# Expert activations of the last 192 tokens as row dot products on VectorE, the dense U product for 384 tokens, in a diff-attention, pooling and PEER layer

## The chip, the cores and the metric

The kernel runs on one core of a Trainium2 chip. The metric is the device time of one execution in microseconds (us); the times shown are of single executions, and their median is what a change is measured by.

## What is computed

One layer of a hybrid decoder for 512 prompt tokens and 64 sample tokens (576 in all, model width 2048): projection, differential attention over a prompt and over paged caches, a pooling branch, gates, output projection, and then the PEER mixer, which the change touches. All numbers are fp32.

```python
def peer_block(h, w_q, sub_keys, u, v):
    N = h.shape[0]
    q = (h @ w_q).reshape(N, PEER_HEADS, 2, PEER_HALF)
    s = jnp.einsum('nhcd,hckd->nhck', q, sub_keys).astype(jnp.float32)
    sv, si = lax.top_k(s, PEER_TOPK)
    cand = (sv[:, :, 0, :, None] + sv[:, :, 1, None, :]).reshape(N, PEER_HEADS, PEER_TOPK * PEER_TOPK)
    cidx = (si[:, :, 0, :, None] * PEER_KEYS + si[:, :, 1, None, :]).reshape(N, PEER_HEADS, PEER_TOPK * PEER_TOPK)
    top_s, top_p = lax.top_k(cand, PEER_TOPK)
    experts = jnp.take_along_axis(cidx, top_p, axis=-1)
    gate = jax.nn.softmax(top_s, axis=-1)
    act = jax.nn.gelu(jnp.einsum('nd,nhkd->nhk', h, u[experts]).astype(jnp.float32), approximate=False)
    return jnp.einsum('nhk,nhkd->nd', (gate * act).astype(h.dtype), v[experts])
```

There are 8 heads, 128 x 128 = 16384 experts, and 16 chosen experts per head, so 128 per token. u and v are 16384 x 2048 (134 MB each). The output is y = h + PEER(norm(h)), normed once more.

## The kernel before

Five engines run programs of their own, written out by hand and joined by semaphores. Every projection multiplies 128-column tiles of a weight with the activations of all tokens. An fp32 product is made of three fp32r ones: weight and activation are split into a rounded part (`w_hi`, `act_hi`; ScalarE casts) and a rest (`w_lo`, `act_lo`; VectorE subtracts), and TensorE adds hi*hi, hi*lo and lo*hi in PSUM.

**Queries.** 16 tiles of `w_peer_q` (`G_PQ`) give the queries `q_ev`; `key_scores` compares each with its sub-keys in fp32, and `best` on VectorE takes the 16 best of 128.

**The U stage.** For all 576 tokens the product with all 16384 rows of u is made, in `N_U` = 128 tiles of 128 experts. Per tile SP loads 1 MB of u into `w_raw` (four DMAs), VectorE transposes it by halves into `turned` (`turn`) and subtracts (`u_low`), ScalarE casts (`u_high`), TensorE runs `expert_tile`: 16 contraction steps, each three products by two halves of 288 tokens, 96 matmuls. ScalarE takes GELU out of PSUM (`gelu`), and SP stores it to `gelu_dram`. Buffers hold two tiles. Beside tiles 0 to 29 VectorE chooses the experts of five token blocks, in pieces that stand between half tiles (`low_half`); TensorE turns the choice (`turn_selected`) so that `iaT`, `ibT`, `gT` hold first index, second index and gate for each token and choice. Beside tiles 30 to 77 the gate matrix of the first `TV` = 384 tokens is made, 8 tokens a tile: VectorE writes one-hots (`one_i`, and `gate_j` twice, with the gate's rounded part and its rest), TensorE multiplies them (`gate_matrix`, 8 matmuls of 256 columns), ScalarE copies and VectorE adds the two parts into `gmat`, and POOL stores it to `gmat_dram` by 32 tokens.

**The value stage.** For 384 tokens the 128 tiles of v are multiplied with GELU times gate (`a_back`, `g_back`), dense, two tiles at a time into `main` (`take_sum`). The last `N_SP` = 192 tokens are done sparsely: POOL gathers for each token its 128 GELU values, one element for each partition (`gather_cells`), and its 128 rows of v (`gather_rows`, 1 MB a token), and TensorE adds up the weighted rows four tokens at a time (`expert_sums`).

Order around the change: VectorE's program is one_hots, merge_gates, u_low and turn, by halves; ScalarE's is u_high of the next tile, GELU, gate copies. At the end of the U stage SP waits for the gate stores, reloads the residual into `main` (whose memory `gmat` shares), loads the first GELU and gate tiles, then v tiles.

```python
def u_low(n, s, i, last=False):
    dve.wait_ge(u_hi, n * 2 + (i + 1))
    v.tensor_sub(w_lo[s][:, 8 * i:8 * i + 8, :], turned[i][:, :, :],
                 w_hi[s][:, 8 * i:8 * i + 8, :].bitcast(F)).then_inc(u_lo, 1)
    if not last:
        dve.wait_ge(u_lo, n * 2 + (i + 1))
        turn(n + 1, 1 - s, i)
```

## Time and profile before

| | us |
|---|---|
| median of 3 executions (4904.4 to 4916.15) | 4909.15 |
| the profiled execution, its own time | 4921.65 |
| its span in the trace | 4919.6 |
| first 30 tiles of the U stage, 1852.5 to 2238.9 | 386.4 |
| tiles 31 to 126, GELU to GELU, 2251.8 to 3526.7 | 1274.9 |
| TensorE busy (matmul) | 4749.3 |
| VectorE busy | 2807.5 |
| ScalarE busy | 1217.3 |
| GpSimd (POOL) busy | 780.0 |

Positions are microseconds from the span's start. A matmul's own duration in a row overlaps with its neighbours', so the time that one takes is read from the distance of the starts. "Idle before" a group and its releaser tell what the engine waited for. The share of DMA is the mean busy share of the 16 DMA engines.

### The profile page before, as it was taken

How to read it: one execution, taken by the hardware profiler on the slowest of the kernel's cores; microseconds unless marked ns; L12 is line 12 of the kernel's file. 1: busy time of each engine (PE TensorE's matmuls, PEld its weight loads, DVE VectorE, ACT ScalarE, POOL GpSimd, SP SyncE). 2: the span in 40 equal slices, each digit the busy share in tenths (PEclk: the TensorE clock that was granted, in tenths of full speed). 3: DMA queues.
4: the chain of work that ended last, by engine and by line, in shares of the span. 5: the costliest groups of instructions: out<-in, count | busy, mean ns of one | idle time of the engine just before them, and what ended most of it. 6: DMA issues, size and time to landing. Idle time of an engine off the chain costs nothing.

```text
span 4919.6 us, 84579 instructions
## 1 busy us (share of the span) xinstructions
PE 4749.3 (97%) x35079; PEld 4510.0 (92%) x35079; DVE 2807.5 (57%) x5183; ACT 1217.3 (25%) x1483; POOL 780.0 (16%) x768
## 2 busy tenths in 40 slices
PE   8999999999999899999999999999999999999997
PEld 8999888888999899999999999999988888888887
DVE  3332643223343668878888863333366666776667
ACT  3212533322121212222222221212222222222223
POOL 1010012320000000000011000000054334434430
PEclk9999999999999999999999999999999999999999
DMA  6333246763445334434555554344488778877873
GB/s 191 104 112 99 64 158 216 235 202 102 134 128 144 71 72 105 109 100 118 131 141 141 133 133 109 102 106 107 162 318 304 303 302 302 310 265 302 305 298 110
DMA packets 474042, 842.18 MB, mean 171 GB/s; under 512 B 45201, under 2 KB 307345, under 8 KB 431512
## 3 DMA queue, kind: packets, MB, share of 16 engines
q1 hardware_dynamic: 400272, 502.55, 33.9%
q0 software_dynamic: 67968, 325.20, 19.0%
q10 hardware_dynamic: 5520, 10.49, 0.7%
q8 instruction: 199, 3.26, 0.3%
q14 instruction: 83, 0.68, 0.0%
HBM read 739.48 MB, written 94.14 MB: 169 GB/s over the span
## 4 chain that ended last, share of the span: by engine, by line
PE 80%; DMA 8%; DVE 6%; issue 3%; ACT 2%; SPq 1%; ACTq 0%; DVEq 0%
PE pair L1795 61%; PE pair L2218 10%; DMA v_raw<-in_peer_v_dram 7%; PE pair L1759 2%; DVE v_lo L1672 2%; PE pair L2199 2%; DVE main L1690 2%; ACT v_hi L1086 1%; PE pair L2152 1%; PE pair L1966 1%; ACT w_hi L776 1%; PE pair L1831 1%; PE pair L2009 1%; SPq L537 0%; PE pair L2106 0%
## 5 line engine op out<-in xcount | busy, mean ns | idle before, releaser
L1795 PE MATMUL pair<-act_hi,w_hi 128*128 128x288 f32 x7616 | 1653.9, 299 | 32.2 <-DVE act_lo L1219 12.1
L1795 PE MATMUL pair<-act_hi,w_lo 128*128 128x288 f32 x7616 | 1635.9, 297 | 0.0
L1795 PE MATMUL pair<-act_lo,w_hi 128*128 128x288 f32 x7616 | 1635.5, 296 | 0.0
L1795 PEld LDWEIGHTS pair<-act_hi,w_hi 128*128 128x128 f32 x7616 | 1229.0, 190 | 71.1 <-issue 64.8
L1795 PEld LDWEIGHTS pair<-act_lo,w_hi 128*128 128x128 f32 x7616 | 1232.9, 190 | 0.0
L1795 PEld LDWEIGHTS pair<-act_hi,w_lo 128*128 128x128 f32 x7616 | 1232.1, 189 | 0.0
L2218 PE MATMUL pair<-wx_hi,v_hi 128*128 128x384 f32 x2016 | 691.0, 343 | 52.7 <-DVE main L1690 44.6
L2218 PE MATMUL pair<-wx_hi,v_lo 128*128 128x384 f32 x2016 | 680.6, 338 | 0.0
L2218 PE MATMUL pair<-wx_lo,v_hi 128*128 128x384 f32 x2016 | 679.9, 337 | 0.0
L1690 DVE TENSOR_TENSOR main<-pair,main 128x384 f32<-128x384 f32 x1024 | 546.3, 553 | 221.5 <-PE pair L2218 206.6
L1159 DVE TENSOR_TENSOR w_lo<-w_raw,w_hi 128x2048 fp32r<-128x2048 f32 x103 | 236.2, 2293 | 749.1 <-ACT w_hi L776 747.4
L1514 DVE TENSOR_TENSOR w_lo<-turned,w_hi 128x1024 fp32r<-128x1024 f32 x256 | 310.4, 1213 | 436.6 <-ACT w_hi L1024 435.7
L2218 PEld LDWEIGHTS pair<-wx_hi,v_hi 128*128 128x128 f32 x2016 | 383.2, 190 | 107.1 <-DVE main L1690 57.5
L776 ACT CAST w_hi<-w_raw 128x2048 fp32r<-128x2048 f32 x112 | 213.5, 1907 | 830.3 <-PE pair L1795 816.4
L1086 ACT CAST v_hi<-v_raw 128x2048 fp32r<-128x2048 f32 x126 | 240.2, 1907 | 688.7 <-DMA v_raw<-in_peer_v_dram 680.6
L1672 DVE TENSOR_TENSOR v_lo<-v_raw,v_hi 128x2048 fp32r<-128x2048 f32 x126 | 288.3, 2288 | 191.0 <-ACT v_hi L1086 188.4
L1030 ACT ACTIVATE tmp<-pair 128x576 f32<-128x576 f32 x128 | 83.5, 652 | 1241.5 <-PE pair L1795 1241.5
L710 POOL DMA_INDIRECT e_rows<-in_peer_v_dram,e_row x192 | 272.1, 1417 | 720.9 <-PE pair L2218 647.6
L2218 PEld LDWEIGHTS pair<-wx_lo,v_hi 128*128 128x128 f32 x2016 | 383.3, 190 | 0.0
L2218 PEld LDWEIGHTS pair<-wx_hi,v_lo 128*128 128x128 f32 x2016 | 382.9, 190 | 0.0
L1509 DVE STREAM_TRANSPOSE turned<-w_raw 128x1024 f32<-128x1024 f32 x256 | 318.7, 1245 | 13.8 <-DVE w_lo L1514 0.2
L1024 ACT CAST w_hi<-turned 128x1024 fp32r<-128x1024 f32 x256 | 256.1, 1052 | 10.9 <-DVE turned L1509 10.9
(294 smaller groups left out, 3402.9 us busy)
## 6 DMA issues: line engine op xcount, KB each, us to landing
w_raw<-in_peer_u_dram SPq DMA_DIRECT2D x512, 256.0 KB
v_raw<-in_peer_v_dram SPq DMA_DIRECT2D x128, 1024.0 KB
w_raw<-in_w_in_dram SPq DMA_DIRECT2D x64, 1024.0 KB
gelu_dram<-tmp SPq DMA_DIRECT2D x128, 288.0 KB, 2.6
gmat_dram<-gmat POOLq DMA_DIRECT2D x24, 1024.0 KB, 11.5
a_back<-gelu_dram SPq DMA_DIRECT2D x128, 192.0 KB
g_back<-gmat_dram SPq DMA_DIRECT2D x128, 192.0 KB
w_raw<-in_w_out_dram SPq DMA_DIRECT2D x16, 1024.0 KB
```

Of the source, the lines that this page charges most:

```text
L710: pool.indirect_dma_start(out=e_rows[b % 2 * COLS + j][:, :], out_offset=None, in_=v_rows, in_offset=bass.IndirectOffsetOnAxis(ap=e_row[:, ...
L776: a.copy(w_hi[g % 2][:, :, :], w_raw[g % 2][:, :, :]).then_inc(hi_done, 1)
L1024: a.copy(w_hi[s][:, 8 * i:8 * i + 8, :], turned[i][:, :, :]).then_inc(u_hi, 1)
L1086: a.copy(value_parts(n)[0][:, :], v_raw[n % 2][:, :]).then_inc(v_hid, 1)
L1159: v.tensor_sub(w_lo[g % 2][:, :, :], w_raw[g % 2][:, :, :], w_hi[g % 2][:, :, :].bitcast(F)).then_inc(lo_done, 1)
L1509: v.transpose(turned[i][:, :, :].rearrange("p k (e c) -> p e k c", c=QR), raw[:, :, 8 * i:8 * i + 8, :]).then_inc(u_turn, 1)
L1514: v.tensor_sub(w_lo[s][:, 8 * i:8 * i + 8, :], turned[i][:, :, :], w_hi[s][:, 8 * i:8 * i + 8, :].bitcast(F)).then_inc(u_lo, 1)
L1672: v.tensor_sub(lo[:, :], v_raw[n % 2][:, :], hi[:, :].bitcast(F)).then_inc(v_lod, 1)
L1690: v.tensor_add(main[:, d, 0:TV], bank(d), main[:, d, 0:TV]).then_inc(acc_done, 1)
L1759: return nc.tensor.transpose(out, in_, ident[0:n, 0:n])
L1795: op = m_(pair[out][:, hf, 0:TH], w[:, k, :], x[:, k, hf * TH:(hf + 1) * TH], start=(starts and k == ks[0] and i == 0), stop=(ends and k = ...
L2218: op = m_(bank(d), w[:, c], x[:, :], start=(start and t == terms[0]), stop=(stop and t == terms[-1]))
```

## The change

The dense U product is made for 384 tokens only: 48 matmuls of 384 columns per tile. To that end the normed activations lie in two pairs of buffers (`h2_hi`, `h2_lo` for tokens 0 to 383, `h2s_hi`, `h2s_lo` for the last 192), and a query tile is 48 times a matmul of 384 and one of 192 columns.

For each of the last 192 tokens POOL gathers its 128 chosen rows of u (1 MB) into one of three buffers `u_rows`, TensorE spreads the token's activation over all partitions of `quad` (four PSUM banks; `ones_r` of two rows times `h_row`, whose two rows are the rounded part and the rest, 512 columns a matmul), and VectorE multiplies and sums: one value of `e_act` per expert (`dot`). ScalarE takes one GELU of `e_act` at the end. Two dots go with each of tiles 31 to 126 (`dots_of`), and every second of these carries a gate matrix of 8 tokens (`group_of`). To have the rows `h_row` in natural order, TensorE turns the split activations beside tiles 0 to 3 (`turn_h`), ScalarE copies (`take_h`) and POOL stores them to `h_dram`. The token blocks are chosen in the order 3, 4, 0, 1, 2. The gate matrix is made of fp32 one-hots, two a token, 8 fp32 matmuls of 128 columns, with no sum on VectorE. POOL's one-element gathers are gone, and the value stage uses the PSUM banks in another order. Loops over tiles are written out.

```diff
+SEL_ORDER = (3, 4, 0, 1, 2)
+SEL_AT = {tb: q for q, tb in enumerate(SEL_ORDER)}
+DOT_TILE = G_FIRST + 1
+U_RING, H_RING = 3, 2
...
+def dots_of(n):
+    return [2 * (n - DOT_TILE) + x for x in range(2)] if 0 <= n - DOT_TILE < N_SP // 2 else []
+def group_of(n):
+    return (n - DOT_TILE) // 2 if 0 <= n - DOT_TILE < 2 * N_G and (n - DOT_TILE) % 2 == 0 else None
...
-            def store_gelu(n, s):
+            def store_gelu(n):
                 sp.wait_ge(a_gelu, n + 1)
-                dst = gelu_dram[n] if isinstance(n, int) else gelu_dram[bass.ds(n, 1)].rearrange("a p t -> p (a t)")
-                sp.dma_start(dst, tmp[:, s, :]).then_inc(a_out[s], 16)
+                sp.dma_start(gelu_dram[n], tmp[:, n % 2, 0:TV]).then_inc(a_out[n % 2], 16)
+            def load_h(i):
+                sp.dma_start(h_row[i % H_RING][:, :].bitcast(F), h_dram[i]).then_inc(h_in[i % H_RING], 16)
...
-            with sp.Fori(2, N_U // 2) as hh:
-                for s in range(2):
-                    sp.wait_ge(u_turn, hh * 4 + 2 * (s - 1))
-                    load_u(hh * 2 + s, s)
-                    store_gelu(hh * 2 + (s - 3), 1 - s)
+            for n in range(N_U - 4):
+                if n:
+                    store_gelu(n - 1)
+                if n == DOT_TILE:
+                    sp.wait_ge(h_saved, H_SAVED + 32)
+                    sp.wait_ge(sel_tev, 3 * TB)
+                    for i in range(H_RING):
+                        load_h(i)
+                for i in dots_of(n)[0:1]:
+                    if i + H_RING < N_SP:
+                        sp.wait_ge(h_spread, i + 1)
+                        load_h(i + H_RING)
+                sp.wait_ge(u_turn, 2 * (n + 3))
+                load_u(n + 4, n % 2)
+                for i in dots_of(n)[1:2]:
+                    if i + H_RING < N_SP:
+                        sp.wait_ge(h_spread, i + 1)
+                        load_h(i + H_RING)
...
-            for b in range(TV // GB):
-                for half in range(2):
-                    t = slice(half * GB // 2, (half + 1) * GB // 2)
-                    to = slice(b * GB + half * GB // 2, b * GB + (half + 1) * GB // 2)
-                    pool.wait_ge(gm_ev, (2 * b + half + 1) * (GB // NTOK_G))
-                    for j in range(0, PK, PK // 2):
-                        pool.dma_start(gmat_dram[:, j:j + PK // 2, to], gmat[:, j:j + PK // 2, t]).then_inc(gm_out[half], 16)
-            def gather_cells(b):
-                for t in batch_tokens(b)[0]:
-                    pool.indirect_dma_start(out=e_act[:, t:t + 1], out_offset=None, in_=gelu_cells,
-                                            in_offset=bass.IndirectOffsetOnAxis(ap=e_cell[:, t:t + 1], axis=0)
-                                            ).then_inc(back_in[b % 4], 16)
+            for b, w in enumerate((P, N_SP - P)):
+                pool.wait_ge(h_ev, H_EV + 4 * (b + 1))
+                pool.dma_start(h_dram[b * P:b * P + w], h_nat[b][0:w, :, :]).then_inc(h_saved, 16)
+            def gather_u(i):
+                if i in (0, P):
+                    pool.wait_ge(top_done, N_PQ + 1 + i // P)
+                pool.indirect_dma_start(out=u_rows[i % U_RING][:, :], out_offset=None, in_=u_rows_dram,
+                                        in_offset=bass.IndirectOffsetOnAxis(ap=e_row[:, i:i + 1], axis=0)
+                                        ).then_inc(u_row_in[i % U_RING], 16)
+            def store_gates(b, half):
+                t = slice(half * GB // 2, (half + 1) * GB // 2)
+                to = slice(b * GB + half * GB // 2, b * GB + (half + 1) * GB // 2)
+                pool.wait_ge(gm_ev, (2 * b + half + 1) * (GB // 2 // NTOK_G))
+                for j in range(0, PK, PK // 2):
+                    pool.dma_start(gmat_dram[:, j:j + PK // 2, to], gmat[:, j:j + PK // 2, t]).then_inc(gm_out[half], 16)
+            for i in range(U_RING):
+                gather_u(i)
+            for n in range(DOT_TILE, N_U):
+                for i in dots_of(n):
+                    if i + U_RING < N_SP:
+                        pool.wait_ge(dot_done, DOT + i + 1)
+                        gather_u(i + U_RING)
+                if group_of(n - 1) is not None and group_of(n - 1) % 4 == 3:
+                    store_gates(*divmod(group_of(n - 1) // 4, 2))
...
+            def take_h(r):
+                b, x, half = r // 4, r // 2 % 2, r % 2
+                w = (P, N_SP - P)[b]
+                act.wait_ge(h_mm, H_MM + r + 1)
+                a.copy(h_nat[b][0:w, x, :].rearrange("t (q k r) -> t k q r", q=NQ, r=QR)[:, 8 * half:8 * half + 8, :, :],
+                       pair[2 + r % 2][0:w, :, :].rearrange("t a (k q r) -> t (a k) q r", q=NQ, r=QR)).then_inc(h_ev, 1)
+            def take_gates(g):
+                t0 = g % (GB // NTOK_G) * NTOK_G
                 act.wait_ge(gm_mm, g + 1)
-                for half in range(2):
-                    a.copy(gate_cells(half, t0), gate_parts(half)[:, 0]).then_inc(gm_cp, 1)
+                if g == 0:
+                    act.wait_ge(h_saved, H_SAVED + 32)
+                if g % 4 == 0 and g >= 8:
+                    act.wait_ge(gm_out[g // 4 % 2], 32 * (g // 8))
+                a.copy(gmat[:, :, t0:t0 + NTOK_G].rearrange("p j (a t) -> p j a t", a=2),
+                       pair[1][:, :, :].rearrange("p a (t j) -> p j a t", j=PK)).then_inc(gm_ev, 1)
...
+            def dot(i):
+                dve.wait_ge(h_spread, i + 1)
+                dve.wait_ge(u_row_in[i % U_RING], U_IN + 16 * (i // U_RING + 1))
+                v.tensor_tensor_reduce(out=u_rows[i % U_RING][:, :], in0=quad[:, :, :].rearrange("p a c -> p (a c)"),
+                                       in1=u_rows[i % U_RING][:, :], scale=1.0, scalar=0.0, op0=ALU.mult, op1=ALU.add,
+                                       accum_out=e_act[:, i:i + 1]).then_inc(dot_done, 1)
+            for n in range(G_FIRST, N_U - 1):
+                g = group_of(n)
+                for part in range(2):
+                    u_low(n + 1, (n + 1) % 2, part, n + 1 == N_U - 1)
+                    if g is not None:
+                        one_hots(g, part)
+                    for i in dots_of(n)[part:part + 1]:
+                        dot(i)
+            dve.wait_ge(gm_mm, N_G)
+            v.tensor_copy(e_gate[:, :], gT[:, TV:T]).then_inc(top_done, 1)
...
+            def query_part(t, k, starts, ends):
+                for i, (w, x) in enumerate(((w_hi, h2_hi), (w_hi, h2_lo), (w_lo, h2_hi))):
+                    for part, nt in enumerate((TV, N_SP)):
+                        op = m_(pair[t % 2][:, part, 0:nt], w[t % 2][:, k, :], x[part][:, k, :],
+                                start=(starts and i == 0), stop=(ends and i == 2))
+                return op
...
-            def expert_tile(n, s, first=False):
-                if not first:
+            def expert_tile(n, hooks):
+                if n >= 2:
                     pe.wait_ge(a_gelu, n - 1)
-                pe.wait_ge(u_lo, n * 2 + 1)
-                tile(w_hi[s], w_lo[s], s, range(8), ends=False)
-                pe.wait_ge(u_lo, n * 2 + 2)
-                tile(w_hi[s], w_lo[s], s, range(8, KD), starts=False).then_inc(a_done, 1)
+                for k in range(KD):
+                    if k % 8 == 0:
+                        pe.wait_ge(u_lo, n * 2 + 1 + k // 8)
+                    if k in hooks:
+                        hooks[k]()
+                    for i, (w, x) in enumerate(((w_hi, h2_hi), (w_hi, h2_lo), (w_lo, h2_hi))):
+                        op = m_(pair[0][:, n % 2, 0:TV], w[n % 2][:, k, :], x[0][:, k, :],
+                                start=(k == 0 and i == 0), stop=(k == KD - 1 and i == 2))
+                op.then_inc(a_done, 1)
+            def spread_h(i):
+                pe.wait_ge(h_in[i % H_RING], H_IN + 16 * (i // H_RING + 1))
+                if i:
+                    pe.wait_ge(dot_done, DOT + i)
+                for c in range(4):
+                    op = m_(quad[:, c, :], ones_r[:, :], h_row[i % H_RING][:, c * 512:(c + 1) * 512], start=True, stop=True)
+                op.then_inc(h_spread, 1)
+            def turn_h(r):
+                b, x, half = r // 4, r // 2 % 2, r % 2
+                w = (P, N_SP - P)[b]
+                if r >= 2:
+                    pe.wait_ge(h_ev, H_EV + r - 1)
+                for k in range(8):
+                    op = tr(pair[2 + r % 2][0:w, k // 4, k % 4 * P:(k % 4 + 1) * P],
+                            (h2_hi, h2_lo)[x][1][:, 8 * half + k, b * P:b * P + w].bitcast(F))
+                op.then_inc(h_mm, 1)
...
-            def gate_matrix(g, s, first=False):
-                pe.wait_ge(oh_v, g + 1)
-                if not first:
-                    pe.wait_ge(gm_ev, g * 2)
+                    pe.wait_ge(sel_tev, 3 * TB)
                 for n in range(NTOK_G):
-                    op = m_(pair[2 + n // 4][:, n // 2 % 2, n % 2 * 2 * PK:(n % 2 + 1) * 2 * PK], one_i[s][:, n, :],
-                            gate_j[s][:, n, :, :].rearrange("p x j -> p (x j)"), start=True, stop=True)
+                    op = m_(pair[1][:, n // 4, n % 4 * PK:(n % 4 + 1) * PK], one_i[g % 2][:, n, :],
+                            gate_j[g % 2][:, n, :], start=True, stop=True)
                 op.then_inc(gm_mm, 1)
...
+            for n in range(N_U):
+                expert_tile(n, {(3, 11)[x]: (lambda i=i: spread_h(i)) for x, i in enumerate(dots_of(n))})
+                q, i = divmod(n, SEL_TILES)
+                if 1 <= q <= TB and i == (1 if q < TB else 0):
+                    turn_selected(SEL_ORDER[q - 1])
+                if n < 4:
+                    turn_h(2 * n)
+                    turn_h(2 * n + 1)
+                if group_of(n) is not None:
+                    gate_matrix(group_of(n))
```

VectorE ahead of a tile with a gate matrix, before (`merge_gates` is L1636; the one-hot rows repeat for four tokens):

```order
L1626 TENSOR_SCALAR gate_j_154<-iota_f,ibT,g_hi 128x128
L1627 TENSOR_SCALAR gate_j_154<-iota_f,ibT,g_lo 128x128
L1514 TENSOR_TENSOR w_lo_57<-turned_159,w_hi_55 128x1024 [waits u_hi]
L1509 STREAM_TRANSPOSE turned_159<-w_raw_52 128x4x8x32 [waits raw_in0,u_lo]
L1625 TENSOR_SCALAR one_i_152<-iota_f,iaT 128x128
```

One-hots stand between every piece, and nothing here waits for TensorE or a gather. In the changed kernel at the first dot tile (`dot` is L1694, a custom instruction and the reading of its accumulator; kp_in0 is the semaphore of the gathered row):

```order
L1570 TENSOR_TENSOR w_lo_65<-turned_169,w_hi_63 128x1024 [waits u_hi]
L1565 STREAM_TRANSPOSE turned_169<-w_raw_62 128x4x8x32 [waits raw_in1,u_lo]
L1685 TENSOR_SCALAR one_i_162<-iota_f,iaT 128x128 [waits sel_tev]
L1686 TENSOR_SCALAR gate_j_164<-iota_f,ibT,gT 128x128
...
L1694 ISA u_rows_54,e_act<-quad,u_rows_54 128x2048 [waits kp_in0,h_spread]
L1694 ISA e_act 128x1
L1570 TENSOR_TENSOR w_lo_65<-turned_170,w_hi_63 128x1024 [waits u_hi]
```

Each half tile is now followed by its one-hots and by a dot, which waits for TensorE and for a gather.

SP's queue in two dot tiles of the changed kernel (before, GELU stores and U loads alone alternate):

```order
L542 DMA h_row_167<-h_dram 2x2048 [waits h_spread]
L539 DMA gelu_dram<-tmp 128x384 [waits a_gelu]
L542 DMA h_row_166<-h_dram 2x2048 [waits h_spread]
L534 DMA w_raw_61<-in_peer_u_dram 32x4x512 [waits u_turn]
L534 DMA w_raw_61<-in_peer_u_dram 32x4x512 x3
```

The second of a tile's two h rows now stands behind the U load.

POOL's queue around a gate store in the changed kernel (x_scaled is the semaphore that counts dots; before, the gate stores stood alone at this point):

```order
L742 DMA u_rows_55<-in_peer_u_dram,e_row 128x2048 [waits x_scaled]
L751 DMA gmat_dram<-gmat 128x64x32 [waits gm_ev]
L751 DMA gmat_dram<-gmat 128x64x32
L742 DMA u_rows_56<-in_peer_u_dram,e_row 128x2048 [waits x_scaled]
L742 DMA u_rows_54<-in_peer_u_dram,e_row 128x2048 [waits x_scaled]
```

Two gate stores now stand between gathers, once in eight tiles.

## Rows read from the trace of the kernel before

**Rows 1.** The page: engine busy (share) x instructions; DMA in 40 slices, tenths.
```profile
PE 4749.3 (97%) x35079; PEld 4510.0 (92%) x35079; DVE 2807.5 (57%) x5183; ACT 1217.3 (25%) x1483; POOL 780.0 (16%) x768
...
DMA   6333246763445334434555554344488778877873
```
**Rows 2.** Busy time by stage: PE, PEld, DVE, ACT, POOL, clock, DMA share, GB/s.
```profile
1852.50:2238.90 386.40, 385.65 (x2889) 385.34 (x2889) 320.51 (x598) 94.12 (x122) 0.00 (x0) 1.00 0.40 105
2251.80:3526.70 1274.90, 1274.90 (x9602) 1274.90 (x9602) 790.12 (x1610) 295.58 (x384) 66.33 (x24) 1.00 0.49 125
3600.00:4800.00 1200.00, 1155.40 (x7008) 1007.44 (x7007) 829.55 (x1268) 277.80 (x231) 473.98 (x452) 0.99 0.79 299
```
**Rows 3.** ScalarE in order of time: GELU after tile 30 and after tile 126.
```profile
2251.83 0.65 ACT L1030 ACTIVATE tmp<-pair 128x576 f32<-128x576 f32 x1 [11.25 <-PE pair L1795]
...
3526.71 0.65 ACT L1030 ACTIVATE tmp<-pair 128x576 f32<-128x576 f32 x1 [10.27 <-PE pair L1795]
```
**Rows 4.** Waits from 1852 to 2239: who for whom, total, times, longest.
```profile
DVE w_lo L1514 <- ACT w_hi L1024: 59.7, 24, 5.6
```
**Rows 5.** TensorE in order of time, value stage: start, duration, instruction.
```profile
4163.28 0.33 PE L2218 MATMUL pair<-wx_hi,v_lo 128*128 128x384 f32 x1
4163.46 0.33 PE L2218 MATMUL pair<-wx_hi,v_hi 128*128 128x384 f32 x1
4163.63 0.33 PE L2218 MATMUL pair<-wx_lo,v_hi 128*128 128x384 f32 x1
```
**Rows 6.** The chain of waits in the query stage: start, us, what.
```profile
1645.25 12.98 PE pair L1795 x96
...
1658.33 1.26 PE pair L2106 x10
```
**Rows 7.** VectorE in order of time, one half tile between one-hots.
```profile
2506.58 0.28 DVE L1625 TENSOR_SCALAR one_i<-iota_f,iaT 128x128 fp32r<-128x128 f32 x1
2506.78 0.34 DVE L1626 TENSOR_SCALAR gate_j<-iota_f,ibT,g_hi 128x128 fp32r<-128x128 f32 x1
2507.03 0.34 DVE L1627 TENSOR_SCALAR gate_j<-iota_f,ibT,g_lo 128x128 fp32r<-128x128 f32 x1
...
2508.00 1.22 DVE L1514 TENSOR_TENSOR w_lo<-turned,w_hi 128x1024 fp32r<-128x1024 f32 x1
2509.25 1.25 DVE L1509 STREAM_TRANSPOSE turned<-w_raw 128x1024 f32<-128x1024 f32 x1
2510.42 0.24 DVE L1625 TENSOR_SCALAR one_i<-iota_f,iaT 128x128 fp32r<-128x128 f32 x1
```
**Rows 8.** ScalarE groups by shape: busy, mean ns, idle before.
```profile
L1024 ACT CAST w_hi<-turned 128x1024 fp32r<-128x1024 f32 x256 | 256.1, 1052 | 10.9 <-DVE turned L1509 10.9
L1048 ACT COPY gmat<-pair 128x512 f32<-128x512 f32 x96 | 51.6, 590 | 13.0 <-PE pair L2152 13.0
```
**Rows 9.** VectorE groups by shape: busy, mean ns, idle before.
```profile
L1559 DVE TENSOR_REDUCE sel<-oh 128x128 f32<-128x2048 f32 x8 | 18.3, 2286 | 0.3
L1418 DVE COPY main<-pair 128x64 f32<-128x64 f32 x8 | 1.8, 225 | 22.6 <-PE pair L1759 22.5
L1196 DVE CUSTOM_DVE_ANT_0 lam_raw<-lam_raw 128x64 f32<-128x64 f32 x2 | 0.4, 220 | 0.0
L1196 DVE DVE_READ_ACCUMULATOR2_ANT lam_v<- 128x1 f32 x2 | 0.2, 82 | 0.0
```
**Rows 10.** DMA queues: packets, MB, share; from 3100 to 3400, 3700 to 4700, 2400 to 2800.
```profile
q1 hardware_dynamic: 16573, 30.92, 39.1%
...
q0 software_dynamic: 26752, 159.48, 42.6%
...
q0 software_dynamic: 3987, 15.41, 18.7%
```
**Rows 11.** DMA share from 3003 to 3013 in 40 slices: GELU store, then U load.
```profile
DMA  0059983555554667595999999563210000000000
```
**Rows 12.** POOL in order of time: the two stores of a half block of gates.
```profile
2517.03 2.76 POOL L698 DMA_DIRECT2D gmat_dram<-gmat  x1 [40.68 <-DVE gmat L1636]
2528.55 2.75 POOL L698 DMA_DIRECT2D gmat_dram<-gmat  x1 [8.76 <-issue]
```
**Rows 13.** DMA issues of the page: count, KB, us to landing.
```profile
main<-hT_dram SPq DMA_DIRECT2D x1, 4032.0 KB, 13.0
```

292 lines of the change are left out of this document (131 added, 161 removed).

## The prediction

> **What bounds the kernel now.** I read the page first. TensorE is busy for 4749 of 4919.6 us and DMA engines rise above half only in the last third [rows 1]. The table by stage [rows 2] splits the part that the change touches: tiles 0 to 29 of the U stage with the expert choice beside them (386.4 us), the other tiles up to 126 (1274.9 us), and the value stage. In the first two PE has no gap at all, VectorE is busy for 320 of 386 and 790 of 1275 us, and DMA has half of its time left. So the dense product sets the U stage. From the first GELU after tile 30 to that of tile 126 [rows 3] 96 tiles take 1274.9 us, 13.28 each (48 carry gate matrices). VectorE lies just below PE in the first 30 tiles: it waits there only 59.7 us for w_hi [rows 4]. The value stage is another regime (PE 1155 of 1200 us, DMA share 0.79), and the change touches it at its ends.
>
> **The shorter product.** A 384-column matmul starts 0.173 us after the one before it [rows 5], 96 of 288 columns take 12.98 us [rows 6]. 48 of 384 columns are 48 x 0.173 = 8.3 us where 12.8 stood. A contraction step (three matmuls) is 0.52 us.
>
> **Tiles 0 to 30.** PE needs 8.3 us a tile, VectorE its present work, so VectorE becomes the bound and its 59.7 us of waits close. PE now trails it directly instead of by a tile's second half: about 10 us more. Light tiles and the first h row give 3 us back: **-67 us**. The h turns (64 transposes) and their eight copies lie beside VectorE's work and cost nothing; without that cover they would be about 7 us of PE.
>
> **One pair of tiles with dots.** Durations: a half tile (w_lo and transpose) 2.42 us, from 2508.00 to 2510.42 [rows 7]; a token's two one-hots 0.20 + 0.25 us by the starts in the same rows, four tokens 1.82 us; the cast 1.05 us, the gate copy of 1024 elements twice 0.59 less overlap, 1.1 us [rows 8]. A dot has no row. Its nearest are the 2048-element reduction, 2.29 us, and the same custom instruction on 64 elements, 0.220 us beside 0.225 us for a copy of 64: element rate as any other, plus 0.08 us to read the accumulator [rows 9]. I take 2.37 us; at half rate it would be 4.4 us, and below 2.3 nothing points. A spread is four 512-column matmuls: adding 128 columns at the 2.4 GHz granted to the 0.173 us gives 0.226, so 0.9 us. A gate matrix is eight fp32 matmuls of 128 columns; ten instructions of that kind take 1.26 us with one narrower pair in it [rows 6], about 0.11 each and two to a matmul, 1.8 us.
> Now the waits. quad is one buffer: a spread waits for the dot before it, a dot for its spread. Let an even tile start on PE at 0. GELU and cast run to 1.55, VectorE's first half to 3.97, one-hots 5.8, dot 8.2. PE is at its second spread at 6.6 and waits until 8.2; spread and five steps bring it to 11.7. VectorE's second half and one-hots end at 12.4; only then can PE make the gate matrix, to 14.2; the second dot ends at 14.8. ScalarE copies the gates and casts until 16.4, so VectorE waits, then half tile 18.8, dot 21.1. PE's second spread in the odd tile waits for that and the tile ends at 24.6. Handoffs of a few hundredths to a tenth, some six on this path, make it 25.3: **12.6 us a tile**, where PE's own work is 11.0 and VectorE's 11.4. Those 12.6 are the floor.
>
> **What DMA adds.** Engine time per MB: 39.1% of 300 us for 30.92 MB of U loads and GELU stores (3.8 us), 42.6% of 1000 us for 159.48 MB of row gathers (2.7), 18.7% of 400 us for 15.41 MB of gate stores (4.9) [rows 10]. Per tile: U and GELU 1.25 MB, 4.7 us; two gathers 2.1 MB, 5.6; gate stores 0.26 MB, 1.3. Together 11.6 us, 92% of 12.6. The value stage averages 0.79. The queues are the issue. SP's second h row of a tile is issued behind the U load, at about 10.6 on the clock above; that load keeps the engines at work for some 6.5 us (slices 6 to 31 of [rows 11]), a gather beside it adds up to 2.7, the row itself 1, so it lands at 19 to 22 and the odd tile's spread wants it at 20.8. I take 0.6 us a tile, bounds 0 and 1.5. The Trainium skill (DMA: Bandwidth & Descriptors, Queues, rings and completion order) says that descriptors on one engine are consumed in ring order and that rows take turns by packet; the order of SP's issues is what makes this speak against the change. By that rule the h row waits out the load and the sum stands as it is; were it not to hold, a tile would take 13.3 us and the time after would be about 4874.
> On POOL two gate stores in a row hold the queue from 2517.03 to 2531.30 [rows 12], and their data follow for some 10 us. A gather behind them lands about 28 us after they began, while the ring of three rows covers 22. This comes once in eight tiles: 0.7 us a tile, bounds 0 and 1.2. So **13.9 us** a tile, 96 x (13.9 - 13.28) = **+60 us**. Bounds: 12.6 (-65) and 15.0 (+165).
>
> **End of the stage.** Tile 127 saves 4 us. The last gate store now leaves at tile 126; the 4 MB load of main overwrites gmat and waits for it, and the first values stand behind that on SP. From the start of tile 126: 25 us for the two stores, 13 for main [rows 13], 2.7 for a v tile, 4.2 for its split: 45, where both tiles are done at 22. **+24 us**, bounds 10 and 30.
>
> **Queries and norm.** A query tile becomes 48 pairs of 384 and 192 columns. 192 has no row: by the slope between 256-288 and 384 columns 0.09 us, by the 128-wide fp32 ones 0.11. That is -0.2 to +0.6 us in each of 16 tiles; with the doubled casts and copies of the norm **+10 us**, bounds 0 and 15. Value-stage removals (192 one-element gathers on POOL, which waits for PE there) cost and gain nothing.
>
> Sum against the profiled execution: 4921.65 - 67 + 60 - 4 + 24 + 10 = 4944. That execution is 12.5 us above the median of the runs, so the median after is **about 4931**, that is 4872 + 96 x (tile time - 13.28).
>
> **Rivals.** (a) *The chain alone decides.* If h rows and gathers land in time, a dot tile takes 12.6 to 13.57 us and the time is 4807 to 4900, faster. For it: each U load has over a tile of slack, and the value stage moves 299 GB/s. It decides where the second h row lands within 10 us of its request. (b) *DMA saturates*: at a mean share near 0.8, as in the value stage, a tile takes 11.6/0.8 = 14.5 and more; 14.3 to 15.0 give 4970 to 5037. Against it: slices there reach 0.9. (c) *The dot runs at half rate*: VectorE then has 30.9 us per pair, 15.7 a tile with handoffs, and 5104. The rows speak against it: 64 elements at half rate would take 0.29 us, not 0.22. The Trainium skill (Vector Engine (DVE) Microarchitecture Reference, Points that are easy to get wrong) says that such an instruction with two fp32 sources in SBUF halves its throughput; the trace's 0.220 us, with both there, does not agree, and here one source is in PSUM. (d) The gain and the queues cancel: 13.57 to 13.77, 4900 to 4919.
>
> **Numbers.** No change means within 0.2%, about what the three runs can tell (4899 to 4919). Forecast, 13.77 to 14.3 us a tile (4919 to 4970): 0.40. (a) 0.32, (b) 0.11, (c) 0.05, (d) 0.12. So faster 0.32, same 0.12, slower 0.56. Low end 4845 (13.0 us a tile leaves 0.1 below), high 5010 (14.7 leaves 0.1 above, (c) among it). The forecast's own range is 4919 to 4970.
>
> **What would show it.** Starts of GELU in tiles 31 to 126: about 1335 us for 96, alternately longer and shorter. PE idle behind the dots and h_row. VectorE busy for over 80% there, DMA share near 0.85. The dot's row at 2.3 us; a row near 4.4 makes (c) right. Tile 30 done some 57 us earlier than now, after queries 10 us longer. A PE gap of 20 us or so ahead of the first value matmuls. If the h rows never end a wait and the tile takes under 13.5 us, the DMA part was wrong; if VectorE waits little and PE's own rows are longer than 0.173 us, the clock or the columns were.

## The result, and the profile after

The changed kernel takes 4985.66 us (median of 4, 4974.09 to 4986.82) where the kernel before takes 4908.96 in the same session: ratio 1.015, 95% interval [1.013, 1.0169], so 77 us slower. The prediction was 4931. Its sign was right and its size was not: +22 forecast, +77 measured. The profiled execution (4985.49 us) lies at the median of its runs, while that of before lay 12.5 us above its own; the two spans differ by 64.1 us, 4983.7 against 4919.6. The terms of the sum are compared on these. One execution of one kernel below (the spread at step 13) took 5498 us at a granted clock of 0.75 and is left out.

The page of the changed kernel, busy time of each engine, the DMA slices, and the row of the dot from its costliest groups:

```profile
PE 4596.4 (92%) x30151; PEld 4199.1 (84%) x30151; DVE 3072.3 (62%) x5114; ACT 1206.3 (24%) x1460; POOL 836.8 (17%) x770
...
DMA  6333156753444335558888889888778888877883
...
L1694 DVE CUSTOM_DVE_ANT_0 u_rows<-quad,u_rows 128x2048 f32<-128x2048 f32 x192 | 436.1, 2271 | 129.7 <-DMA u_rows<-in_peer_u_dram,e_row 119.4
```

Against [rows 1] TensorE has 153 us less to do and still the kernel is longer. DMA stands at 8 and 9 from the first dot on. The dot takes 2.27 us and 0.08 more for its accumulator, 2.35 together where 2.37 were taken; VectorE is idle for 129.7 us ahead of dots, and 119.4 of them are waits for a gathered row.

Busy time by stage of the changed kernel (PE, PEld, DVE, ACT, POOL, granted clock, DMA share, GB/s), the answer to [rows 2]: tiles 0 to 30, tiles 31 to 126, value stage.

```profile
1867.80:2193.40 325.60, 280.40 (x1518) 270.30 (x1517) 316.28 (x561) 99.04 (x125) 4.73 (x5) 0.95 0.53 133
2193.40:3584.20 1390.80, 1232.31 (x6150) 1085.44 (x6148) 1059.68 (x1536) 277.14 (x339) 310.51 (x212) 0.91 0.86 248
3619.30:4983.70 1364.40, 1291.11 (x7796) 1130.83 (x7796) 953.56 (x1453) 333.87 (x308) 310.83 (x288) 0.98 0.75 285
```

The granted clock has fallen from 1.00 to 0.91 in the dot tiles. ScalarE in order of time gives the ends of the stages, as [rows 3] did: GELU of tile 30, of tile 126, and of tile 127, which now stands behind the first values; after them, from TensorE in order of time, its first matmul on v.

```profile
2193.45 0.49 ACT L1083 ACTIVATE tmp<-pair 128x384 f32<-128x384 f32 x1 [3.21 <-PE pair L2196]
...
3584.21 0.49 ACT L1083 ACTIVATE tmp<-pair 128x384 f32<-128x384 f32 x1 [8.11 <-PE pair L2196]
...
3619.07 0.48 ACT L1083 ACTIVATE tmp<-pair 128x384 f32<-128x384 f32 x1
```
```profile
3619.31 0.98 PE L2288 MATMUL pair<-first_x,first_hi 128*128 128x384 f32 x2 [26.81 <-ACT first_hi L1136]
```

With tile 0's GELU at 1867.8 (before: 1865.2) and the first value matmul at 3619.3 (before: 3539.3), the span's 64.1 us are:

| stretch | predicted | measured |
|---|---|---|
| up to tile 0's GELU | +10 | 1867.8 - 1865.2 = +2.6 |
| tiles 0 to 30 | -67 | 325.6 - 386.6 = -61.0 |
| tiles 31 to 126 | +60 | 1390.8 - 1274.9 = +115.9 |
| tile 126 to the first value matmul | -4 + 24 = +20 | 35.1 - 12.6 = +22.5 |
| value stage to the end | 0 | 1364.4 - 1380.3 = -15.9 |

One stretch failed by 56 us: a dot tile takes 14.49 us where 13.9 were predicted. The distances between GELUs there are not even: 12.8 and 13.7 (or 12.1 and 13.2) in turn, and once in eight tiles 23 to 26 us; that is ten times, and at the first store the loss is spread over two tiles (21.1 and 18.4). The waits in that stretch (who for whom, total, times, longest), of those on TensorE and VectorE:

```profile
DVE w_lo L1570 <- ACT w_hi L1077: 194.6, 85, 4.3
...
PE quad L2206 <- DVE e_act L1694: 146.8, 46, 11.8
...
DVE u_rows L1694 <- DMA u_rows<-in_peer_u_dram,e_row: 119.4, 11, 12.8
...
PE quad L2206 <- DMA h_row<-h_dram: 10.6, 3, 6.5
```

Eleven waits for a gather, one to each of these places. POOL in order of time at one of them, and behind it the chain of waits through the same place:

```profile
2660.67 2.82 POOL L751 DMA_DIRECT2D gmat_dram<-gmat  x1
2676.43 2.79 POOL L751 DMA_DIRECT2D gmat_dram<-gmat  x1 [12.94 <-issue]
2679.53 1.01 POOL L742 DMA_INDIRECT u_rows<-in_peer_u_dram,e_row  x1 [0.31 <-issue]
```
```profile
2679.53 14.15 DMA u_rows<-in_peer_u_dram,e_row
...
2696.26 2.04 PE quad L2206 x4
2698.30 7.13 PE pair L2196 x24
```

POOL stands idle for 12.94 us ahead of the second gate store (8.76 in [rows 12], with DMA half idle), and the gather behind it lands 14.15 us after its issue, at 2693.68: 33.0 us after the stores began, where the prediction had 28. The dot that wants this row waits for 11.2 us, so the ring covered 21.8, as predicted (22). At all eleven places POOL's idle time is 12.4 to 14.0 us. Then TensorE needs 7.13 us for 24 matmuls that take 4.39 elsewhere (5.7 to 7.2 at the eleven places).

The slower matmuls are the other surprise, and they are in most pairs of tiles. TensorE in order of time in an even tile, around the second spread, and behind it the table by stage in pieces of 2 us:

```profile
2612.89 0.34 PE L2196 MATMUL pair<-h_hi,w_lo 128*128 128x384 f32 x1
2614.29 1.17 PE L2206 MATMUL quad<-h_row,ones_r 2*128 2x512 f32 x4 [1.06 <-DVE e_act L1694]
...
2616.43 0.53 PE L2196 MATMUL pair<-h_hi,w_hi 128*128 128x384 f32 x1
2616.76 0.53 PE L2196 MATMUL pair<-h_lo,w_hi 128*128 128x384 f32 x1
...
2619.15 0.34 PE L2196 MATMUL pair<-h_hi,w_hi 128*128 128x384 f32 x1
2619.32 0.34 PE L2196 MATMUL pair<-h_lo,w_hi 128*128 128x384 f32 x1
```
```profile
2612.00:2614.00 2.00, 1.23 (x8) 0.91 (x6) 2.00 (x1) 0.00 (x0) 0.00 (x0) 1.00 1.04 339
2614.00:2616.00 2.00, 1.71 (x6) 1.27 (x7) 1.97 (x4) 0.00 (x0) 1.58 (x1) 0.88 0.79 329
2616.00:2618.00 2.00, 2.00 (x7) 2.00 (x7) 2.00 (x8) 0.00 (x0) 0.09 (x1) 0.50 0.66 124
```

The spread waits 1.06 us for the dot, and in the two microseconds that follow it the granted clock (third number from the end) is 0.50, that is 1.2 GHz, where it had been 1.00: the starts lie 0.32 us apart instead of 0.17, until about 2618.7. The 15 matmuls take 4.38 us instead of 2.84, so 1.06 us of waiting are followed by a loss of 1.5 more. (A packet is booked where it begins, so a short stretch can show a DMA share above 1.)

### The profile page after: what moved, and what is told of

It reads as the page before. It is cut to its first block, busy times and chain, and to the rows that moved or that the text cites. A ratio compares the mean times of both kernels' runs of the same rounds, so it can differ in the third digit from the quotient of the medians.

```text
span 4983.7 us, 71732 instructions
## 1 busy us (share of the span) xinstructions
PE 4596.4 (92%) x30151; PEld 4199.1 (84%) x30151; DVE 3072.3 (62%) x5114; ACT 1206.3 (24%) x1460; POOL 836.8 (17%) x770
## 4 chain that ended last, share of the span: by engine, by line
PE 58%; DVE 16%; DMA 12%; issue 8%; ACT 3%; POOL 2%; SPq 1%; ACTq 0%; DVEq 0%
PE pair L1836 22%; PE pair L2288 10%; PE pair L2196 8%; DMA v_raw<-in_peer_v_dram 8%; PE pair L2155 4%; DMA u_rows<-in_peer_u_dram,e_row 3%; DVE w_lo L1570 3%; PE quad L2206 2%; DVE u_rows L1694 2%; DVE v_lo L1713 2%; PE quad L1836 2%; PE quad L2269 2%; DVE main L1731 2%; PE pair L2239 1%; ACT v_hi L1136 1%
## 5 line engine op out<-in xcount | busy, mean ns | idle before, releaser
L2196 PE MATMUL pair<-h_hi,w_hi 128*128 128x384 f32 x2048 | 751.0, 367 | 48.3 <-DVE w_lo L1570 48.1
L2196 PE MATMUL pair<-h_hi,w_lo 128*128 128x384 f32 x2048 | 723.0, 353 | 0.0
L2196 PE MATMUL pair<-h_lo,w_hi 128*128 128x384 f32 x2048 | 722.9, 353 | 0.0
L1836 PE MATMUL pair<-act_hi,w_hi 128*128 128x288 f32 x2752 | 606.9, 302 | 16.8 <-DVE act_lo L1489 8.3
L1836 PE MATMUL pair<-act_hi,w_lo 128*128 128x288 f32 x2752 | 591.8, 297 | 0.0
L1836 PE MATMUL pair<-act_lo,w_hi 128*128 128x288 f32 x2752 | 591.2, 297 | 0.0
L1694 DVE CUSTOM_DVE_ANT_0 u_rows<-quad,u_rows 128x2048 f32<-128x2048 f32 x192 | 436.1, 2271 | 129.7 <-DMA u_rows<-in_peer_u_dram,e_row 119.4
L1836 PEld LDWEIGHTS pair<-act_hi,w_hi 128*128 128x128 f32 x2752 | 443.4, 190 | 51.3 <-issue 47.0
L1836 PEld LDWEIGHTS pair<-act_lo,w_hi 128*128 128x128 f32 x2752 | 445.6, 190 | 0.0
L1836 PEld LDWEIGHTS pair<-act_hi,w_lo 128*128 128x128 f32 x2752 | 445.5, 190 | 0.0
## 6 DMA issues: line engine op xcount, KB each, us to landing
v_raw<-in_peer_v_dram SPq DMA_DIRECT2D x128, 1024.0 KB, 11.5
```

Source lines behind the costliest of these rows:

```text
L1694: v.tensor_tensor_reduce(out=u_rows[i % U_RING][:, :], in0=quad[:, :, :].rearrange("p a c -> p (a c)"), in1=u_rows[i % U_RING][:, :], scal ...
L1836: op = m_(pair[out][:, hf, 0:TH], w[:, k, :], x[:, k, hf * TH:(hf + 1) * TH], start=(starts and k == ks[0] and i == 0), stop=(ends and k = ...
L2196: op = m_(pair[0][:, n % 2, 0:TV], w[n % 2][:, k, :], x[0][:, k, :], start=(k == 0 and i == 0), stop=(k == KD - 1 and i == 2))
```

## The experiments

Every kernel is compared by its ratio to the kernel before, run on the same chip in the same session (medians of before: 4921.8, 4916.8, 4909.4, 4910.7 and 4912.8 us in the five sessions). "96 tiles" is the distance of the GELUs of tiles 30 and 126 in the trace: 1274.9 before, 1390.8 after. It holds one start-up interval of 21 to 24 us, so two or three microseconds between kernels say nothing.

### The gate stores: split, and made small

```diff
-                for j in range(0, PK, PK // 2):
-                    pool.dma_start(gmat_dram[:, j:j + PK // 2, to], gmat[:, j:j + PK // 2, t]).then_inc(gm_out[half], 16)
+                for j in pieces:
+                    pool.dma_start(gmat_dram[:, j:j + PK // 8, to], gmat[:, j:j + PK // 8, t]).then_inc(gm_out[half], 16)
...
-                if group_of(n - 1) is not None and group_of(n - 1) % 4 == 3:
-                    store_gates(*divmod(group_of(n - 1) // 4, 2))
+                m = n - DOT_TILE - 7
+                if m >= 0:
+                    q, i = divmod(m, 8)
+                    store_gates(*divmod(q, 2), [PK // 8 * i] if n < N_U - 1 else range(PK // 8 * i, PK, PK // 8))
```

> The changed kernel with the gate stores in eight pieces of 128 KB to a tile each instead of two of 1 MB once in eight tiles; bytes, packets and queue (POOL) are the same. Theory A (the two stores hold POOL's queue, and gathers behind them come late: 11 waits of a dot for a gather, 119.4 us): the waits and the half clock behind them go, no tile takes over 16 us, 4986 - 120 to 135 = 4850 to 4870. Theory B (the stores cost by their packets on full DMA engines, wherever they stand): the lateness is spread over all tiles, ordinary tiles go from 13.1 to 14 us or more, time 4960 to 4990.

Measured: 4856.4 us, ratio 0.9879 [0.9856, 0.9902]: 129 us less than the changed kernel by the medians and 133 by the ratios, and faster than the kernel before. 96 tiles take 1263.9 us and no tile over 15 behind the start-up.

In the small-store kernel the stores stay where the changed kernel has them, and each writes one column instead of 64 (`gmat[:, j:j + 1, t]`); the value stage reads the stored columns, so its result is not the layer's.

> The changed kernel with gate stores of 1/64 of the columns (the rest of the gate matrix is not stored, and the value stage reads stored columns instead; the arithmetic is all made). Both theories: the twelve long tiles go, 4986 - 135 = 4850, and the end of the stage is 10 to 20 us shorter for want of the last store: 4830 to 4840. Theory A: ordinary tiles stay at 13.0 to 13.2 us. Theory B (full DMA engines): the ordinary tiles, which have 0.26 MB less to move each in the mean, fall under 12.8 us, and the time is under 4815.

Measured: 4843.5 us, ratio 0.9842 [0.9825, 0.9858]; 96 tiles 1260.9 us, 3 less than with all bytes in eight pieces, which is within the start-up's scatter. From the GELU of tile 126 to the first value matmul it takes 16.5 us instead of 31.1: most of the longer end of the stage is the wait for the last gate store. The waits of the split kernel from 2200 to 3400 us, and behind them its line of the table by stage (columns as above):

```profile
PE quad L2208 <- DVE e_act L1696: 45.9, 43, 1.1
...
PE quad L2208 <- DMA h_row<-h_dram: 11.9, 3, 8.9
```
```profile
2200.00:3400.00 1200.00, 1143.15 (x5843) 1006.01 (x5844) 1006.56 (x1465) 262.71 (x319) 342.74 (x266) 0.95 0.92 275
```

No dot waits for a gather any more, though the DMA share has risen to 0.92. So it was where the bytes stood, not their number. A wait of 1.1 us in nearly every pair stays, and so does the low clock (0.95).

The split kernel also shows what the clock costs by itself. Two pairs in a row, with the same wait of 1.07 us ahead of the second spread: each spread on TensorE with its wait, the lines of the table by stage behind each, and ScalarE's GELUs, of which the first, third and fifth end a pair.

```profile
2737.06 1.16 PE L2208 MATMUL quad<-h_row,ones_r 2*128 2x512 f32 x4 [1.07 <-DVE e_act L1696]
...
2763.58 1.15 PE L2208 MATMUL quad<-h_row,ones_r 2*128 2x512 f32 x4 [1.07 <-DVE e_act L1696]
```
```profile
2738.00:2742.00 4.00, 4.00 (x15) 3.85 (x15) 3.96 (x11) 0.00 (x0) 0.89 (x1) 0.65 0.92 278
2764.00:2768.00 4.00, 3.86 (x21) 3.13 (x20) 3.97 (x11) 0.41 (x1) 1.41 (x1) 1.00 0.88 258
```
```profile
2728.96 0.49 ACT L1085 ACTIVATE tmp<-pair 128x384 f32<-128x384 f32 x1 [8.11 <-PE pair L2198]
2742.57 0.49 ACT L1085 ACTIVATE tmp<-pair 128x384 f32<-128x384 f32 x1 [11.24 <-PE pair L2198]
2755.48 0.49 ACT L1085 ACTIVATE tmp<-pair 128x384 f32<-128x384 f32 x1 [8.14 <-PE pair L2198]
2767.59 0.49 ACT L1085 ACTIVATE tmp<-pair 128x384 f32<-128x384 f32 x1 [9.74 <-PE pair L2198]
2780.80 0.49 ACT L1085 ACTIVATE tmp<-pair 128x384 f32<-128x384 f32 x1 [8.11 <-PE pair L2198]
```

Behind the first wait the clock falls and the pair takes 26.52 us; behind the second it stays at 1.00 and the pair takes 25.32. Of the 47 pairs from tile 33 on, 31 have such a fall and a median of 26.5 us, 16 have none and take 25.3. The wait itself is in both kinds, so it costs nothing at the end of the pair; the half clock costs 1.15 us, 31 times.

### The h rows ahead of the U load

```diff
+                for i in dots_of(n)[1:2]:
+                    if i + H_RING < N_SP:
+                        sp.wait_ge(h_spread, i + 1)
+                        load_h(i + H_RING)
                 sp.wait_ge(u_turn, 2 * (n + 3))
                 load_u(n + 4, n % 2)
-                for i in dots_of(n)[1:2]:
...
```

> The changed kernel with a tile's second h row requested ahead of the U load instead of behind it. The prediction's term (0.6 us a tile, 58 us in all, for h rows behind U loads): 4986 - 58 = 4928. Against it the profile after the change, where the spreads wait for h rows 10.6 us in three places: then 4970 to 4990, no change.

> The kernel with split gate stores and a tile's second h row requested ahead of the U load. By the prediction's term of 0.6 us a tile it falls by 58 us to 4798; by the waits of the run with split stores, 12 us in three places, it stays within 4840 to 4860.

Measured: 4974.1 us alone, ratio 1.0112 [1.0095, 1.0129] against 1.015 [1.013, 1.0169]: the intervals just fail to overlap, a gain of 12 us by the medians and 19 by the ratios; with split stores 4851.0, ratio 0.9873 [0.9855, 0.9891], no difference from 0.9879. At most a third of the term of 0.6 us a tile (58 us) is there in the changed kernel, and nothing of it once the stores are split.

### The second spread later

```diff
-                expert_tile(n, {(3, 11)[x]: (lambda i=i: spread_h(i)) for x, i in enumerate(dots_of(n))})
+                expert_tile(n, {(3, 14)[x]: (lambda i=i: spread_h(i)) for x, i in enumerate(dots_of(n))})
```

> The changed kernel with one edit: the second spread of a dot tile stands at contraction step 14 instead of 11, so that TensorE still has matmuls while VectorE finishes the first dot. Theory A (the spread's wait for the dot, and the half clock of TensorE behind it, set the ordinary tiles): in the changed kernel a pair of tiles takes 26.5 us, with 1.06 us of waiting at that spread and 15 matmuls at 0.29 instead of 0.19 us (1.5 us); without both a pair takes 24 to 25.5 us and the time falls from 4986 by 50 to 120 us, to 4866 to 4936; granted clock in the dot tiles above 0.95. Theory B (the DMA engines are full, share 0.86, and set the pace): the pair stays at 26 us or more, the waits turn up at gathers and h rows, time 4965 to 4990.

Measured: 4994.0 us, ratio 1.0155 [1.0138, 1.0171], no gain. Theory A failed as it was put: the spread's waits for dots fell to 54.5 us, but dots now waited 86.7 us for spreads and spreads 47.5 us for h rows. With split stores, h rows first and the spread at step 13:

> Split gate stores, h rows ahead of the U load, and the second spread at contraction step 13. With the spread at 14 alone spreads waited 47 us for h rows and dots 87 us for spreads; if those came from the order on SP, they go here, the wait for the dot and the half clock go too, and the time is 4780 to 4810. If the later spread only moves the wait to the second dot and the gate matrix behind it, it is 4840 to 4870.

Measured: 4835.8 us (4817.7, 4835.8 and 4836.2), ratio 0.9838 [0.9817, 0.9859], between the two expectations; the first of these is the profiled one. The clock is at 0.99 from 2195 to 3440 us, and TensorE waits for one-hots ahead of gate matrices instead:

```profile
PE pair L2241 <- DVE gate_j L1688: 53.6, 46, 1.6
```

These 46 waits of 1.17 us in the mean are as long as those at the spread, and the clock falls behind none of them. Tiles go 11.1 and 14.3 us in turn, 25.3 a pair, as the split kernel's pairs without a fall.

### Work in the place of the wait

```diff
+            def filler(n, x):
+                if x == 1 and group_of(n):
+                    pe.wait_ge(gm_ev, group_of(n))
+                    for _ in range(7):
+                        m_(pair[1][:, 0, 0:TV], w_hi[n % 2][:, 10, :], h2_hi[0][:, 10, :], start=True, stop=True)
```

> The kernel with split gate stores (4856 us), and in each tile with a gate matrix seven more matmuls of 384 columns ahead of the spread at step 11, into a bank that is rewritten afterwards: TensorE works for about 1.2 us where it waited 1.06 us for the dot. If the half clock behind that wait comes from the wait and costs 1.5 us in each of 48 pairs, the granted clock stays at 1.00 and the time falls by 50 to 72 us, to 4784 to 4806, though work was added. If the clock does not matter, the time stays or rises by up to 12 us: 4850 to 4870.

> Split stores, the seven more matmuls where TensorE waited, and h rows ahead of the U load. The two edits are independent if the waits for h rows (19 us with the filler alone) go: 4817 - 5 to 15 = 4802 to 4812.

The filler stands ahead of the second spread of a tile with a gate matrix, in 47 tiles (the first has none). Measured: 4817.1 us, ratio 0.9797 [0.978, 0.9815]: 39 us less than with split stores, by adding 329 matmuls whose product nobody reads. That is 11 us above the range for a fall in each of 48 pairs. With h rows first 4816.0, ratio 0.9805 [0.9789, 0.9822], the same. The table by stage, 2200 to 3400 us, filler kernel:

```profile
2200.00:3400.00 1200.00, 1193.86 (x6346) 1044.64 (x6347) 1035.52 (x1499) 270.96 (x329) 354.79 (x275) 0.99 0.95 283
```

The clock is 0.99 and tiles go 12.2 and 13.1 us in turn, 25.3 a pair. The wait itself was only filled, so the gain is the clock's: 35.7 us over the 96 tiles (1228.2 against 1263.9). It is what the 31 pairs with a fall lose in the split kernel (31 times 1.15); the others had nothing to win.

### Is it DMA? The gathers left out

```diff
-                for i in dots_of(n):
-                    if i + U_RING < N_SP:
-                        pool.wait_ge(dot_done, DOT + i + 1)
-                        gather_u(i + U_RING)
```

> Split gate stores, and no gathers of U rows but the first three; the dots multiply those rows again and write into PSUM, and so the expert activations of 192 tokens are not computed. 200 MB less to move, DMA share from 0.91 to about 0.5. If the chain of waits between VectorE and TensorE sets the ordinary tiles, they stay at 12.8 to 13.1 us and the time at 4840 to 4860; if the full DMA engines do, tiles fall below 12.6 us and the time below 4815.

> Split stores, filler matmuls and h rows ahead of the U load (4816 us, pairs of 12.2 and 13.1 us), without the gathers of U rows but the first three; the dots write into PSUM. Is that version bound by the chain of TensorE and VectorE or by DMA (share 0.94)? By the chain: pairs stay at 25.3 us and the time at 4805 to 4825. By DMA: under 4790.

The kernel is the one with split stores; the dots multiply the three rows again and write into PSUM. Measured: 4862.4 us, ratio 0.9887 [0.9868, 0.9905], against 0.9879 with all gathers; and 4820.7, ratio 0.9816 [0.9799, 0.9833], against 0.9805. The same line of the first:

```profile
2200.00:3400.00 1200.00, 1145.65 (x5853) 1008.62 (x5852) 1010.54 (x1457) 262.71 (x319) 101.07 (x88) 0.95 0.50 117
```

The DMA share falls from 0.92 to 0.50 and the time does not move. The chain between TensorE and VectorE (dot, spread, matmuls, gate matrix, GELU, cast, half tile, one-hots, dot) sets the tile, not the DMA engines that are 92% busy.

### The dots left out

```diff
-                v.tensor_tensor_reduce(out=u_rows[i % U_RING][:, :], in0=quad[...], in1=u_rows[...], ..., accum_out=e_act[:, i:i + 1])
+                v.tensor_tensor(e_act[:, i:i + 1], quad[:, 0, 0:1], u_rows[i % U_RING][:, 0:1], ALU.mult)
```

> Split stores, and each dot replaced by one product of a single column (so the expert activations of 192 tokens are not computed); spreads, gathers, one-hots and gate matrices stay. VectorE then has 6.8 us of work a tile and TensorE is the bound. By the prediction its own work is 11.0 us a tile, by the rows of the changed kernel 11.9 (spreads of 1.12 and a slower matmul behind each): time 4856 - 96 x (13.1 - 11.9) = 4740 by the rows, 4655 by the prediction, if DMA keeps up; not under 4760 if the DMA engines bound a tile at 12 us.

> Split stores, each dot replaced by one product of a single column (the expert activations of 192 tokens are not computed), and h rows ahead of the U load. Without that edit it took 4856 us: tiles of 11.0 and 12.8 us in turn, and every few tiles one of 14 to 17, with 65 us of waits for h rows (0.68 us a tile). If those come from SP's order, all tiles take 11.9 us in the mean and the time is 4856 - 96 x 1.2 = 4740 (4730 to 4760). If the DMA engines are the bound at 12.5 to 13 us a tile, it stays above 4790.

> As the run without dots and with h rows ahead of the U load (4906 us, waits of 101 us for h rows that landed after 18 us), and without the gathers of U rows but the first three (neither dots nor gathers, so no expert activations of 192 tokens). If the late h rows there came from DMA engines asked for more than they can move in 11.9 us a tile, nothing is late now, all tiles alternate 11.0 and 12.8 us, granted clock 1.00, and the time is 4906 - 96 x (13.6 - 11.9) = 4740, bounds 4725 to 4765. If TensorE's own chain makes them late, it stays above 4800.

Measured: 4856.2 us (ratio 0.9882 [0.986, 0.9904]), with h rows first 4906.0 (0.9987 [0.9972, 1.0001]), and without gathers too 4751.2 (0.967 [0.9652, 0.9687]). Taking some 2.2 us from each of 192 VectorE operations gained nothing (4740 was expected if DMA keeps up, 4760 or more if it does not). Most tiles do go 11.0 and 12.8 us in turn, the 11.9 of TensorE's own rows, but in between one takes 14 to 24. The chain of waits of the second kernel shows how; behind it the line from 2200 to 3400 us of the second kernel and of the third:

```profile
2964.97 17.50 DMA h_row<-h_dram
2982.48 0.04 issue
2982.52 2.07 PE quad L2206 x4
2984.59 6.32 PE pair L2196 x24
2990.91 1.12 PE quad L2206 x4
```
```profile
2200.00:3400.00 1200.00, 1093.25 (x5639) 960.60 (x5638) 599.67 (x1229) 253.60 (x308) 330.65 (x257) 0.94 0.94 265
```
```profile
2200.00:3400.00 1200.00, 1174.82 (x6291) 1036.98 (x6290) 670.24 (x1363) 285.17 (x344) 111.73 (x98) 0.99 0.54 132
```

At 11.9 us a tile the kernel asks for 0.92 x 13.1 = 12.1 us of packet time (split kernel), more than there is. Three stretches of 12 us around the place above (columns as before) show it:

```profile
2912.00:2924.00 12.00, 12.00 (x69) 10.58 (x69) 5.05 (x6) 3.40 (x4) 3.05 (x3) 1.00 0.97 258
...
2960.00:2972.00 12.00, 12.00 (x69) 10.58 (x68) 5.05 (x6) 3.39 (x4) 4.78 (x5) 1.00 1.04 298
...
2984.00:2996.00 12.00, 12.00 (x57) 10.77 (x56) 4.47 (x12) 0.49 (x1) 3.85 (x3) 0.80 0.45 138
```

The share is 0.97 to 1.04 from 2912 on, and the last piece of a U load lands after 11.5, 12.8 and then 19.4 us: a backlog. Then a row of 16 KB, requested at 2964.97, lands 17.5 us later; TensorE stands still, runs at half clock behind it, the share drops to 0.45, and it begins anew. Without the gathers no tile does so (11.9 us a tile). So DMA is the bound once the chain would go under some 12.1 us a tile (an estimate, from 0.92 x 13.1; at 12.7, in the filler kernel, it was not). The mean share of 0.94 hides it, since it is made of full stretches and of empty ones behind each late row; for the same reason these kernels reach only 13.0 and 13.7 us a tile. Requesting the h rows earlier made it worse (4906 against 4856); why is open.

### Two stores apart, and two orders that were to be better

```diff
-                if group_of(n - 1) is not None and group_of(n - 1) % 4 == 3:
-                    store_gates(*divmod(group_of(n - 1) // 4, 2))
+                m = n - DOT_TILE - 7
+                if m >= 0:
+                    q, i = divmod(m, 8)
+                    if n == N_U - 1:
+                        store_gates(*divmod(q, 2), [PK // 2])
+                    elif i % 4 == 0:
+                        store_gates(*divmod(q, 2), [PK // 8 * i])
```

> The changed kernel with its two gate stores of 1 MB apart: the first in the tile where both stood, the second four tiles later, gathers between them. In the changed kernel the second store was issued 12.9 us after the first had been, and the gathers stood behind both. If the lateness comes from two stores in a row (the second waits for room in the queue), one store alone holds a gather up by at most 14 us, which the ring of three rows (two dot times of slack, about 20 us) covers: time as with eight pieces, 4850 to 4870. If one store is already enough, two shorter stalls of about 3 to 6 us stand in eight tiles: 4900 to 4950.

> The kernel with the two gate stores four tiles apart (5032 us), with the second h row requested ahead of the U load. There spreads waited 102 us for h rows and dots 97 us for spreads. If a gate store of 1 MB costs because the h row stands behind the U load on SP while the store's packets fill the engines, these waits go, the long tiles of 20 us fall to 13 to 15, and the time is 4850 to 4890. If a burst of 1 MB delays whatever is under way, h rows ahead of the U load come late too: 4960 to 5030.

Measured: 5032.2 us, ratio 1.0239 [1.0214, 1.0264]; with h rows first 4915.9, ratio 1.0009 [0.9989, 1.0028]. The first is worse than the changed kernel, which neither expectation held. Its chain of waits behind one store begins with an h row:

```profile
2972.95 14.22 DMA h_row<-h_dram
2987.21 1.82 PE quad L2211 x4
2989.03 5.11 PE pair L2201 x15
```

POOL had begun the store at 2961.35. No gather is late now, but the second h row, requested 0.5 us behind a U load, lands after 14.22 us, and a tile takes 18 to 23 us, twice in eight tiles instead of once 25. At all 22 waits of this kind from 2300 us on the store had begun 24 to 27 us before the spread. Ahead of the U load the time is 116 us less and spreads wait 68.7 us for h rows instead of 116.5; the long waits that stay are half as many and stand at no fixed distance from a store. So in one piece a store of 1 MB and a U load together make a small transfer late; what the store does alone is not shown. In eight pieces neither happens.

The gate matrix a tile after its one-hots, with the spreads at steps 3 and 13, 7 and 14 (first) or 3 and 14, 6 and 11 (second), split stores and h rows first:

```diff
-                if group_of(n) is not None:
-                    gate_matrix(group_of(n))
+                if group_of(n - 1) is not None:
+                    hooks[10] = lambda g=group_of(n - 1): gate_matrix(g)
```

> Split stores, h rows ahead of the U load, spreads at steps 3 and 13 in tiles with one-hots and at 7 and 14 in the others, and the gate matrix in the tile after its one-hots (step 10), its copy after that tile's GELU. With the spread at 13 alone, TensorE waited 54 us for the one-hots ahead of gate matrices; if only the chain between the engines counts, nothing waits now, VectorE's work (11.4 us a tile) and TensorE's (11.9) set the tile: 96 x (12.65 - 12.0) = 60 us less than with the filler, 4750 to 4770. If the DMA engines (share 0.94 there) are the next bound, waits for gathers and U loads appear and it stays at 4790 to 4830.

> As the run with the gate matrix a tile later, with spreads at steps 3 and 14 in tiles with one-hots and 6 and 11 in the others, the gate matrix at 9. There a spread waited 0.9 us for a dot in each pair (44 us), and TensorE ran at half clock behind it (mean 0.96). If those two are what kept a pair at 25 to 26.4 us, it is 23.8 to 24.4 us now and the time 4750 to 4775, granted clock 0.99. If DMA (share 0.92 there) is the bound, waits for h rows, gathers or U loads take their place: 4800 to 4850.

Measured: 4856.9 us (4838.4 to 4883.9), ratio 0.9905 [0.9875, 0.9934], and 4878.9, ratio 0.9935 [0.9918, 0.9951]. Both missed the time hoped for by 80 us and more, and both lie above the other range too. Part of it is the end of the stage: the last gate matrix and its store come a tile later, and from tile 126 to the first value matmul it takes 42 us instead of 31. The rest is in the tiles. In the second kernel a spread waits for a dot twice in a pair instead of once; its tiles take 11.5 and 15.3 us at a clock of 0.95. Its waits from 2200 to 3400 us:

```profile
PE quad L2208 <- DVE e_act L1696: 55.8, 87, 0.9
```

The two are of 0.42 and 0.86 us (spreads at 2915.29 and 2921.70). Behind the first the clock stays at 1.00, behind the second it is 0.50 from 2924 to 2926 us. In the whole stretch it fell behind none of 45 waits of the first kind and behind 30 of 44 of the second; a pair with a fall takes 26.8 us, one without 25.2. Both expectations took an order of steps without such waits for granted, and a wait of under 1 us can cost more than it lasts. Of the kernels that compute the whole layer, the fastest are those with split stores and the filler, 4816 and 4817 us, 2% under the kernel before.

## Why the prediction was wrong

**What was right.** The dot (2.37 us with its read, measured 2.27 and 0.08), and with it the fall of rival (c). For two sources in SBUF that are not bf16 the Trainium skill (Vector Engine (DVE) Microarchitecture Reference, Points that are easy to get wrong) has half the rate, of one shape of instruction; whether this custom instruction has that shape no trace tells. Here one source lies in PSUM, and the only rows with both in SBUF are the two of 64 elements in [rows 9], which do not show half rate. Tiles 0 to 30 (-61 for -67). The end of the stage (+22.5 for +20): the first g_back is waited for 27.0 us behind the last store, as described, and with small stores the end shrinks by 14.6 us. The sign, too.

**What was right in part by luck.** The chain of 25.3 us a pair is the measured one, 25.3, where the clock does not fall. But its path was not quite this: TensorE's own work is 11.9 us a tile (neither dots nor gathers) and not 11.0, since a spread takes 1.12 us and not 0.9 and the first matmul behind it starts later; and the wait drawn in the odd tile is not there, TensorE waits for a dot only in the one with the gate matrix.

**The step that failed: the gate stores on POOL, "0.7 us a tile, bounds 0 and 1.2".** They cost 1390.8 - 1263.9 = 127 us over 96 tiles, 1.32 a tile, above the upper bound. The mechanism was named with its place; the size came from [rows 12], two stores on engines that were half idle. On engines at 0.86 POOL was idle for 12.94 us ahead of the second issue instead of 8.76, and the row came after 33 instead of 28. The ring's 22 us were right, so the lateness was 11 us instead of 6, eleven times, and TensorE lost 1.4 to 2.8 us more behind each at half clock.

**The term that was missing: the clock.** The sum priced TensorE's waits by their length alone. Behind two in three of them TensorE runs at 1.2 GHz for a while: 35.7 us over the 96 tiles by the filler run and by the two kinds of pairs, 0.37 a tile. [rows 2] show 1.00 in both U stretches, with TensorE busy throughout; that the change creates the first waits was in the prediction, that they slow what follows was not. The Trainium skill (TensorE: Matmul & The Clock Gate, What's actually happening) has the throttled state as the default which activity releases. The fall from 1.00 to 0.50 behind a wait of 1.06 us agrees; why 46 waits of 1.17 us ahead of gate matrices had none behind them stays open.

**The term that was too high: h rows behind U loads, 0.6 us a tile.** Spreads waited 10.6 us for them in all. In the changed kernel asking for them earlier gained 12 to 19 us, with split stores nothing. This hid part of the error: 12.6 + 0.6 + 0.7 = 13.9 was predicted, and 12.7 (filler run, 1228.2 us less its start-up, over 95) + 0.4 (clock and wait) + 1.3 (stores) = 14.4 found, where the whole stretch gives 14.49 with the start-up. The mechanism shows where the two gate stores stand apart: 116.5 us of waits for h rows behind the U load, 68.7 ahead of it. The start-up of tile 31 (21 us instead of 14) was not seen either.

**Rivals.** The time lay in the band of (b), DMA saturated, but not for its reason: the same bytes in other places gave 129 us back, and from there 200 MB less to gather changed nothing. Its time for saturation was also too high; DMA becomes the bound at some 12.1 us (the estimate above), not 14.5. (a) is the nearest in kind: the chain does decide, at 13.0 us with the clock and 12.7 without, once nothing holds the gathers; at 4856 us that kernel lies in the band of (a).

**The rest.** The value stage was 15.9 us shorter where nothing was predicted. Its one-element gathers are gone and its banks are in another order, but these may have nothing to do with it: in the profiled executions of the seventeen other kernels of this document, all with the changed value stage, it takes 1364 to 1384 us, and the 1380.3 of before lies among them. The remaining 13 us between 64 and 77 come from the sample: the 12.5 us by which the profiled execution of before lay above its median were carried over to the changed kernel, whose profiled execution had none.

## What to carry to other kernels

A large store issued in one piece on the queue that feeds a short ring must be priced at the DMA load that the change will bring, against the ring's slack; cut into a piece per tile, the same bytes were free here at a DMA share of 0.92. A wait of TensorE is priced with what runs behind it at half clock: here the wait was covered and the clock was not, so that work nobody needs in its place made the kernel faster. Where such falls come and go in one trace, compare the stretches with and without. And a mean DMA share of 0.9 says nothing by itself: leave the bytes out and see whether the time moves, both in the kernel as it is and in the one where the other bound is gone, and read the share in short stretches.

## What was not expected of the hardware

- Waits of TensorE for a dot ahead of a spread (matmuls with two rows of input) were followed by a granted clock of 0.50 in some cases and not in others of the same length: 28 of 44 of about 1.07 us (split kernel), 30 of 44 of 0.86 us and none of 45 of 0.42 us (the last kernel above).
- The wait's length is not all: behind 46 waits of 1.17 us in the mean ahead of gate matrices (spread at step 13) the clock never fell, though it did behind 9 of 23 of 1.4 us with the spread at step 14, close to other waits. What decides was not tried.
- A second store of 1 MB in short packets was issued 12.94 us after the first had been, on POOL, with nothing that the profile names as the cause; with 128 KB pieces an issue took 1.2 us and none waited behind another.
- A row of 16 KB took 14.2 us to land, requested 0.5 us behind a U load and 11.6 us after a 1 MB store of another queue had begun, and 17.5 us under overload.
- The mean DMA share of an overloaded stretch was only 0.94: 0.97 to 1.04 in the 12 us stretches ahead of a late row, 0.45 behind it.
